# Seven products of quarter sums for 44 weight units of the two retention layers

## The chip, the cores and the metric

One core of one Trainium2 chip. The metric is the device time of one execution in microseconds; 1887.9 is the median of three runs of the kernel before (1887.67 to 1889.9).

## What is computed

512 tokens of width 1024 go through one block of differential attention, gated convolution and a feed-forward part, and then through two retention layers. Only the retention layers are touched:

```python
for layer in range(DEPTH_2):                                   # 2
    h = rms_norm(x, pre_norm[layer])
    proj = jnp.einsum("bsd,dp->bsp", h, w_in[layer])            # 1024 -> 8192
    c_b, c_c, c_x, c_z, r_q, r_k, r_v, r_z = jnp.split(proj, cuts, axis=-1)
    y_conv = c_b * causal_depthwise_conv(c_c * c_x, conv_w[layer])
    y_conv = y_conv * jax.nn.silu(c_z)
    q = apply_rotary(r_q...); k = apply_rotary(r_k...); v = r_v...
    ret = retention_chunkwise(q, k, v, log_gamma)
    ret = ret * lax.rsqrt(jnp.mean(ret * ret, axis=-1, keepdims=True) + NORM_EPS)
    y_ret = ret.reshape(b, s, D_RET) * jax.nn.silu(r_z)
    mix = jnp.concatenate([y_conv, y_ret], axis=-1)
    x = x + rms_norm(jnp.einsum("bse,ed->bsd", mix, w_out[layer]), post_norm[layer])
```

All of it is float32.

## The kernel before

Every large matrix product is done with split operands: a float32 value is written as a high part (a rounded copy, made by ScalarE) and a low part (the value less its high part, made by VectorE), and a product is the three matmuls high x high, high x low and low x high, with operands of 128 x 128 (held) and up to 128 x 512 (moving).

**Weights.** `plan` lists units of 1024 x 256 weights, each loaded by SyncE in one DMA of 1 MB into one of three buffers RAW. A unit is cut into slots (BY_COL: two halves of 128 columns; BY_K: two halves of 512 rows). `split_hi` (ScalarE) and `split_lo` (VectorE) make a slot's two parts in WHI and WLO, of which there are three places, taken in turn. A slot can be split once the slot that had its place before is `done`. `fill(upto)` splits as many slots as can be; `take` gives the next slot and fills two ahead. `load(u + 3)` follows the last split of unit u. Every queue is in order, and the order of the program is the order of each queue.

**A retention layer** is `layer(l)`, with four passes over p, each for two heads and 256 conv channels. A pass has three phases:
- q and k: `two_tiles` makes two tiles of 128 columns x 512 tokens each; ScalarE swaps halves into SW, VectorE does the rotation (two products and a sum per tile). In the first pass of the second layer `halves_qk` does this together with the end of the layer before.
- v and gate z (`fin`): 4 token tiles x 256 columns each, held operand the tokens, moving operand the weights; ScalarE writes VTK and SZ.
- The conv phase: kinds x, c, b, z, for each two tiles of 128 columns x 512 tokens, each tile read from PSUM by VectorE as soon as it is made. After each tile stands a piece of the attention (`pieces`: scores, states, mix_values, turn_back, in the second layer also turn_residual), and the elementwise work of the conv tile is emitted right behind it. Its result MXF is split at once into MXH and MXL; those of the attention are split in `turn_back`.

After the fourth pass the output projection multiplies MXH and MXL (`mix_out`, in the second layer `last_out`). `loose` is a list of small steps which are emitted at set points (`loose_run(n)`). PSUM has 8 banks, which turn over three roles.

The inner loop of a tile is in `products` (line 400), one matmul per instruction. A unit of two tiles is 2 x 8 x 3 = 48 matmuls of 512 moving columns; a unit of v or z is 96 of 256.

Of the kernel before, what the change touches and what calls it, by code (L numbers as in the profile page):

```python
# [52 lines left out]
def bass_diff_attention_block_then_retention_layers_kernel(  # L53
# [13 lines left out]
    KT = 8  # L67
# [13 lines left out]
    with ctx:  # L81
# [31 lines left out]

        con = [o_con]
# [75 lines left out]
        def mm(after, o, w, m, start, stop_, mark=False):  # L190
            return pe.put(after, lambda e: e.matmul(o, w, m, start=start, stop=stop_), mark)  # L191

# [100 lines left out]
        swaps, extra = [(1, 2)], {}  # L293
        for l in range(2):
            wl = w_in_2[l]
            for j in range(4):
                for g in (4, 5, 6, 7):
                    unit(cols(wl, 1024 * g + 256 * j), BY_K)
                for g in (2, 1, 0, 3):
                    unit(cols(wl, 1024 * g + 256 * j), BY_COL)  # L300
            if l == 0:
# [3 lines left out]


                n = sum(len(ss_) for _, ss_ in plan)
                extra[n - 1] = extra[n + 3] = 3
                swaps.append((n + 1, n + 2))
            else:  # L310
                for k in range(0, 16, 2):
                    unit(cols(w_out_2[l], 0, k, 2, 1024), [(0, 1, 0, 1024), (1, 2, 0, 1024)])

        raw_count = [Count(sem(f"raw{i}")) for i in range(3)]
        loaded, slots = [], []
# [5 lines left out]
        place = []  # L321
        for s in range(len(slots)):
            place.append(extra[s] if s in extra else (s - sum(e < s for e in extra)) % 3)
        before = [max((r for r in range(s) if place[r] == place[s]), default=None) for s in range(len(slots))]
        extra_free = []
        ready, gone = [], []

        def load(u, after):
            src = plan[u][0]
            n = src.shape[1] * src.shape[2]  # L330
            dst = RAW[u % 3][:, 0:n].rearrange("p (k c) -> p k c", k=src.shape[1])
            t = sp.dma(after, dst, src, raw_count[u % 3])
            loaded.append({k: t for k in range(src.shape[1])})

        def load_half(u, half):
# [4 lines left out]
            if half[0] == 0:  # L340
                loaded.append({})
            loaded[u][half[0]] = t

        halves = []

        def split_hi(s):
            u, (k0, k1, c0, c1), _ = slots[s]
            src = plan[u][0]
            n = (k1 - k0) * (c1 - c0)
            raw = RAW[u % 3][:, 0:src.shape[1] * src.shape[2]].rearrange("p (k c) -> p k c", k=src.shape[1])  # L350
            raw = raw[:, k0:k1, c0:c1]
            hi = WHI[place[s]][:, 0:n].rearrange("p (k c) -> p k c", k=k1 - k0)
# [4 lines left out]
            halves.append((hi, lo, raw, act([loaded[u][k0], used], hi, raw, ACT.Copy)))  # L357

        def split_lo(s):
            u, _, last = slots[s]  # L360
# [3 lines left out]
            if last and u + 3 < len(plan):  # L364
                load(u + 3, [t_lo])
# [14 lines left out]
        def fill(upto):  # L380
            while len(ready) < min(upto, len(slots)) and (before[len(ready)] is None or before[len(ready)] < len(gone)):
                split(len(ready))

        def fill_hi(upto):

            while len(halves) < min(upto, len(slots)) and (before[len(halves)] is None or before[len(halves)] < len(gone)):
                split_hi(len(halves))

        def done(token):
            gone.append(token)  # L390
# [84 lines left out]
        def whole():  # L475
# [953 lines left out]
            MXH = at("mxh", [128, 16, T2], R, o_c)  # L1429
            MXL = at("mxl", [128, 16, T2], R, o_c + 32768)  # L1430
# [56 lines left out]
            def layer(l):  # L1487
# [40 lines left out]
                def final_norm(f, a):  # L1528
                    t_pa[0] = t_x[f] = stt([a, t_x[f], t_w, xtok[f]], H[:, f, NM:T1], H[:, f, NM:T1], cv[:, f, WFIN:WFIN + 1], SUM4, ALU.mult, ALU.mult)
# [5 lines left out]
                mtok = [None] * 16  # L1535
                qk_used, vz_used, xa_used = {}, [], [dg_read, dg_read]
                sw_used = [extra_done, extra_done]

                for p in range(4):

                    b1, b2, b3 = roles
                    b4 = [6, 7]
# [496 lines left out]
```

How the kernel before makes its waits and increments, by code:

```python
    def play(self, eng):  # L41
        reached = {}
        for after, emit, sem, by in self.ops:
            for count, value in after:
                if reached.get(id(count), 0) < value:
                    eng.wait_ge(count.sem, value)
                    reached[id(count)] = value
            instruction = emit(eng)
            if by:
                instruction.then_inc(sem, by)
# [1933 lines left out]
        @block.sync  # L1984
        def _(eng):
            sp.play(eng)
            for count, value in finished:
                eng.wait_ge(count.sem, value)
```

## Time and profile before

| | us |
|---|---|
| runs, median of three | 1887.9 (1887.67 to 1889.9) |
| profiled execution, span | 1885.5 |
| one full pass of the first layer | 97.36 |
| its phases: q and k / v and z / conv | 22.36 / 22.74 / 52.26 |
| one full pass of the second layer | 98.23 |

The span is the time from the first to the last instruction of the profiled execution. The median of the runs is 2.4 us longer. A stage's TensorE time is read from the window table (busy time of each engine in a stretch); a matmul's pace is read from the starts of its neighbours in the list of instructions in order of time, since the matmuls overlap and their ends are modelled. The same holds for VectorE and ScalarE: a record runs on a little while the next one starts. Some matmul records may be missing.

### The profile page before, as it was taken

To read this page: it belongs to the slowest core of one execution; us is meant where nothing else is said; L and a number is where in the kernel's file an instruction comes from. 1 tells how busy PE (TensorE), PEld (TensorE's weight loads), DVE (VectorE), ACT (ScalarE), POOL (GpSimd) and SP (SyncE) were. 2 spreads that over 40 slices of the span, in tenths; PEclk is the share of its full clock that TensorE was granted. 3 is DMA by queue.
4 is the path that set the end of the run, shared out by engine and by line. 5 is a ranking of instruction groups with operands and counts; after the bars stand their busy time and mean duration, and the time that the engine had idled before them with its cause. 6 is when DMAs were issued, how large, how long until landed. Compare 5 with 4: busy or idle time off the path is not lost.

```text
span 1885.5 us, 28594 instructions
## 1 busy us (share of the span) xinstructions
PE 1867.1 (99%) x12262; PEld 1688.0 (90%) x12262; DVE 1130.1 (60%) x2035; ACT 737.5 (39%) x1379; POOL 1.2 (0%) x9
## 2 busy tenths in 40 slices
PE   8999999999999999999999999999999999999998
PEld 7999999877899988998898989898899898989887
DVE  5888897577657753666746363636266636454534
ACT  6222333677634432344433333333245333333322
POOL 0000000000000000000000000000000000000000
PEclk9999999999999999999999999999999999999999
DMA  5222222101222223223323233322333232223131
GB/s 185 94 90 90 71 94 87 64 24 46 68 73 92 95 89 107 90 78 94 107 83 102 78 90 90 89 90 80 100 90 90 73 96 78 90 71 108 68 123 45
DMA packets 151837, 163.64 MB, mean 87 GB/s; under 512 B 3495, under 2 KB 148192, under 8 KB 151711
## 3 DMA queue, kind: packets, MB, share of 16 engines
q1 hardware_dynamic: 151694, 161.82, 27.1%
q8 instruction: 96, 1.57, 0.3%
q14 instruction: 31, 0.25, 0.0%
q10 hardware_dynamic: 16, 0.00, 0.0%
HBM read 159.71 MB, written 2.10 MB: 86 GB/s over the span
## 4 chain that ended last, share of the span: by engine, by line
PE 98%; ACT 1%; DVE 1%; DMA 0%; issue 0%; SPq 0%; DVEq 0%
PE ps L191 95%; PE ps L196 2%; ACT nhi L199 0%; DMA xt<-in_x_dram 0%; ACT p L199 0%; DVE ast L973 0%; ACT L199 0%; DVE p L210 0%; DVE wlo L202 0%; ACT whi L199 0%; DVE m L202 0%; ACT ps L199 0%; DVE ga L210 0%; SPq L38 0%; ACT rbc L199 0%
## 5 line engine op out<-in xcount | busy, mean ns | idle before, releaser
L191 PE MATMUL ps<-nhi,whi 128*128 128x256 f32 (+3 forms) x2528 | 682.2, 319 | 3.6 <-DVE nlo L202 2.1
L191 PE MATMUL ps<-nhi,wlo 128*128 128x256 f32 (+3 forms) x2528 | 673.4, 316 | 0.0
L191 PE MATMUL ps<-nlo,whi 128*128 128x256 f32 (+2 forms) x2400 | 637.6, 318 | 0.0
L202 DVE TENSOR_TENSOR wlo<-raw,whi 128x1024 fp32r<-128x1024 f32 (+2 forms) x308 | 365.0, 1189 | 349.7 <-ACT whi L199 349.1
L191 PEld LDWEIGHTS ps<-nhi,whi 128*128 128x128 f32 x2528 | 426.2, 189 | 35.8 <-DVE nlo L202 2.3
L191 PEld LDWEIGHTS ps<-nhi,wlo 128*128 128x128 f32 x2528 | 425.5, 189 | 32.2
L191 PEld LDWEIGHTS ps<-nlo,whi 128*128 128x128 f32 x2400 | 400.8, 189 | 29.1
L199 ACT ACTIVATE whi<-raw 128x1024 fp32r<-128x1024 f32 (+2 forms) x308 | 314.6, 1026 | 261.4 <-PE ps L191 261.0
L210 DVE SCALAR_TENSOR_TENSOR c<-u,cv,c 128x514 f32<-128x514 f32 x240 | 163.2, 748 | 0.0
L191 PE MATMUL ps<-wlo,nhi 128*128 128x256 f32 x512 | 81.6, 281 | 0.0
L191 PE MATMUL ps<-whi,nhi 128*128 128x256 f32 x512 | 81.6, 281 | 0.0
L191 PE MATMUL ps<-whi,nlo 128*128 128x256 f32 x512 | 81.3, 281 | 0.0
L199 ACT ACTIVATE y<-zr,cf 128x512 f32<-128x512 f32 x44 | 35.8, 816 | 113.4 <-DVE zr L202 113.4
L191 PEld LDWEIGHTS ps<-whi,nhi 128*128 128x128 f32 x512 | 70.0, 189 | 0.6
L191 PEld LDWEIGHTS ps<-wlo,nhi 128*128 128x128 f32 x512 | 69.8, 189 | 0.0
L191 PEld LDWEIGHTS ps<-whi,nlo 128*128 128x128 f32 x512 | 69.6, 189 | 0.0
L191 PE MATMUL ps<-alo,whi 128*128 128x512 f32 x176 | 68.5, 389 | 0.0
L191 PE MATMUL ps<-ahi,whi 128*128 128x512 f32 x176 | 68.5, 389 | 0.0
L191 PE MATMUL ps<-ahi,wlo 128*128 128x512 f32 x176 | 68.5, 389 | 0.0
L210 DVE SCALAR_TENSOR_TENSOR y<-zr,cf,y 128x512 f32<-128x512 f32 x88 | 65.9, 748 | 1.8 <-ACT y L199 0.3
L207 DVE TENSOR_SCALAR nx<-ss 128x4 f32<-128x4 f32 (+2 forms) x26 | 4.3, 164 | 102.6 <-ACT ones_d L199 93.9
L199 ACT ACTIVATE ones_d<-ps,osc 128x128 f32<-128x128 f32 x64 | 23.5, 368 | 93.5 <-PE ps L191 91.9
(267 smaller groups left out, 2171.7 us busy)
## 6 DMA issues: line engine op xcount, KB each, us to landing
raw<-in_w_in_dram SPq DMA_DIRECT2D x90, 1024.0 KB, 5.5
raw<-in_w_up_dram SPq DMA_DIRECT2D x22, 1024.0 KB, 5.0
raw<-in_w_out_dram SPq DMA_DIRECT2D x20, 1024.0 KB, 5.1
raw<-in_w_down_dram SPq DMA_DIRECT2D x8, 768.0 KB, 4.9
raw<-in_w_down_dram SPq DMA_DIRECT2D x8, 640.0 KB, 4.6
raw<-in_w_conv_out_dram SPq DMA_DIRECT2D x4, 1024.0 KB, 5.2
xt<-in_x_dram SPq DMA_DIRECT2D x4, 512.0 KB, 5.5
raw<-in_w_in_dram SPq DMA_DIRECT2D x4, 512.0 KB, 8.2
```

Source lines behind the costliest of these rows:

```text
L191: return pe.put(after, lambda e: e.matmul(o, w, m, start=start, stop=stop_), mark)
L196: return pe.put(after, lambda e: e.transpose(o, i, idn), mark)
L199: return ac.put(after, lambda e: e.activation(o, i, func, **kw))
L202: return dv.put(after, lambda e: e.tensor_tensor(o, a, b, op))
L207: return dv.put(after, lambda e: e.tensor_scalar(o, a, s1, s2, op0, op1))
L210: return dv.put(after, lambda e: e.scalar_tensor_tensor(o, a, s, b, op0, op1))
```

## The change

In both layers the units of q and k (but for the first pass) and of x, c, b and z are multiplied as two-by-two blocks: the 1024 rows in two halves (four blocks of 128 each), the 256 columns in two halves, and the 512 tokens in two halves. Seven products of 512 rows x 128 columns with 256 tokens, of sums of weight quarters with sums of token quarters, and sums of their results give the four result quarters. 44 units are done so: 4 + 6 + 6 + 6 in each layer. The units of v and gate z, and q and k of each first pass, stay as they are.

- A unit of this kind has four slots: SEVEN. One (`0:8, 0:128`) is split as it is loaded. For the others `quarter_sums` first makes four sums on VectorE, three of them in place in RAW, one in S1T. One slot (place 4, WHI[4]) has half size. The places are written out by hand (`place`) in place of taken in turn.
- S1T, WHI[4] and WLO[4] lie in the third RAW buffer, so in the retention layers two RAW buffers are left, and a load follows the last split of the unit before it in its buffer.
- `token_sums` makes, once a layer, four combinations of the token quarters, TF, splits them into THI and TLO; `final_norm` waits for these as it overwrites H.
- `seven` emits the products over three banks: A takes four products and B one and C two, with accumulation carried on over what the bank already holds. Between products ScalarE copies the bank to SBUF (s1, u2, k5, u3, c21) and VectorE joins (c11, c22, c12). Two sets of three banks alternate; the attention has banks 6 and 7.
- Results of a unit now lie in SBUF, not in PSUM. The elementwise work of q, k and the conv kinds, also the rotation, is cut into steps in `loose`, and is emitted two steps at a time in `hook(m)` after each product; the attention's pieces stand at fixed hooks (`pieces`, key 7n + m).
- MXF shares its memory with the token sums, so mixed tiles stay float32 until the end of the last pass. `mix_split` makes their MXH and MXL: 8 tiles in z of the fourth pass, 8 at the start of the output projection.

The core of the diff:

```diff
+        SEVEN = [(0, KT, 0, 128, 0), (0, 4, 0, 128, 1), (0, 4, 0, 256, 2), (4, 8, 0, 256, 3)]
+        SEVEN_AT = [0, 4, 1, 2]
...
+        def quarter_sums(u):
...
+            w11, w21, w12, w22 = raw[:, 0:4, 0:128], raw[:, 0:4, 128:256], raw[:, 4:8, 0:128], raw[:, 4:8, 128:256]
+            t1 = tt([loaded[u][0], summed.get("split"), ready[-1][2]], S1T, w21, w22, ALU.add)
+            t3 = tt([t1], w21, w11, w21, ALU.add)
+            t2 = tt([t1, t3], w11, w11, S1T, ALU.add)
+            t4 = tt([t2], w12, w12, w11, ALU.add)
+            summed[u] = {1: t1, 2: [t2, t3], 3: t4}
...
+                    t = product(A, ah[:, 0:4, :], al[:, 0:4, :], ta, direct(0, TWO[0]), True, True, claim(banks[0]))
+                    s1 = act([t, after[0]], d11, A, ACT.Copy)
+                    hook(0)
+                    t = product(B, ah[:, 4:8, :], al[:, 4:8, :], ta, direct(1, TWO[0]), True, True, claim(banks[1]))
+                    done(t, s0)
+                    c11 = tt([t, s1], d11, B, d11, ALU.add)
+                    release(c11, banks[1])
+                    fill(s0 + 8)
+                    hook(1)
+                    t = t_used[0] = product(A, bh[:, :, left], bl[:, :, left], tb, summed_(0), False, True, s1)
+                    u2 = act([t], d12, A, ACT.Copy)
+                    hook(2)
+                    t = t_used[1] = product(C, ch, cl, tc, summed_(1), True, True, claim(banks[2]))
+                    done(t, s0 + 1)
+                    k5 = act([t, after[1]], d22, C, ACT.Copy)
+                    fill(s0 + 8)
+                    hook(3)
+                    t = t_used[2] = product(A, bh[:, :, right], bl[:, :, right], tb, summed_(2), False, True, u2)
+                    done(t, s0 + 2)
+                    u3 = act([t], d21, A, ACT.Copy)
+                    c22 = stt([k5, u3], d22, d22, -1.0, d21, ALU.mult, ALU.subtract)
+                    fill(s0 + 8)
+                    hook(4)
+                    t = product(C, dh[:, :, left], dl[:, :, left], td, direct(1, TWO[1]), False, True, k5)
+                    c12 = tt([t, u2], d12, C, d12, ALU.add)
+                    release(c12, banks[2])
+                    hook(5)
+                    t = t_used[3] = product(A, dh[:, :, right], dl[:, :, right], td, summed_(3), False, True, u3)
+                    done(t, s0 + 3)
+                    c21 = act([t, c22], d21, A, ACT.Copy, scale=-1.0)
+                    release(c21, banks[0])
+                    fill(s0 + 8)
+                    hook(6)
...
+                def mix_split(*ks):
+                    for k in ks:
+                        a = act([t_mx[k], t_used[k // 4]], MXH[:, k, :], MXF[:, k, :], ACT.Copy)
+                        mtok[k] = [a, tt([a], MXL[:, k, :], MXF[:, k, :], MXH[:, k, :].bitcast(F), ALU.subtract)]
...
+                    pieces = {1: lambda: scores(0), 4: lambda: states(0), 8: lambda: mix_values(0), 12: lambda: scores(1),
+                              15: lambda: states(1), 18: lambda: turn_back(0), 20: lambda: mix_values(1), 26: lambda: turn_back(1)}
...
+                        return [meet, tap0, lambda: tap(1), lambda: tap(2)]
...
+                        return [scale, gate, meet, last]
```

`product` does for k in 0 to 3 the three matmuls of 256 columns. `meet`, `tap(1)`, `tap(2)`, `scale`, `last` are VectorE, `tap0` and `gate` ScalarE.

## Rows read from the trace of the kernel before

**Rows 1.** The page: span, busy time and share, and the chain by engine.
```profile
span 1885.5 us, 28594 instructions
PE 1867.1 (99%) x12262; PEld 1688.0 (90%) x12262; DVE 1130.1 (60%) x2035; ACT 737.5 (39%) x1379; POOL 1.2 (0%) x9
...
PE 98%; ACT 1%; DVE 1%; DMA 0%; issue 0%; SPq 0%; DVEq 0%
```

**Rows 2.** Window table: a full pass, its phases; v/z of both layers' first pass.
```profile
core 0: us, PE busy (x) PEld busy (x) DVE busy (x) ACT busy (x) POOL busy (x), PEclk, DMA share, GB/s
937.51:962.04 24.53, 24.53 (x210) 24.52 (x208) 16.87 (x22) 9.91 (x19) 0.00 (x0) 1.00 0.35 106
...
1111.66:1134.02 22.36, 22.36 (x100) 18.11 (x98) 13.28 (x17) 9.10 (x13) 0.00 (x0) 1.00 0.39 113
1134.02:1156.76 22.74, 22.74 (x194) 22.74 (x192) 8.64 (x10) 8.33 (x17) 0.00 (x0) 1.00 0.31 95
1156.76:1209.02 52.26, 52.26 (x264) 43.74 (x263) 26.66 (x62) 16.94 (x37) 0.00 (x0) 1.00 0.24 73
...
1419.46:1443.09 23.63, 23.63 (x203) 23.63 (x202) 17.79 (x40) 11.80 (x22) 0.00 (x0) 1.00 0.28 84
...
1111.66:1209.02 97.36, 97.36 (x553) 84.59 (x552) 48.58 (x89) 34.38 (x65) 0.00 (x0) 1.00 0.29 87
```

**Rows 3.** TensorE in order of time: 256-column matmuls.
```profile
1134.02 0.63 PE L191 MATMUL ps<-whi,nhi 128*128 128x256 f32 x4
...
1145.38 0.64 PE L191 MATMUL ps<-whi,nhi 128*128 128x256 f32 x4
...
1372.03 0.28 PE L191 MATMUL ps<-mxh,wlo 128*128 128x256 f32 x1
...
1372.75 0.28 PE L191 MATMUL ps<-mxh,wlo 128*128 128x256 f32 x1
```

**Rows 4.** VectorE in order of time: starts of neighbouring operations.
```profile
1185.67 1.22 DVE L202 TENSOR_TENSOR wlo<-raw,whi 128x1024 fp32r<-128x1024 f32 x1
1186.81 0.69 DVE L202 TENSOR_TENSOR sd<-ps,far 128x512 f32<-128x512 f32 x1
1187.41 0.68 DVE L202 TENSOR_TENSOR pa<-ps,xa 128x512 f32<-128x512 f32 x1
...
1206.45 0.69 DVE L202 TENSOR_TENSOR xa<-xa,pa 128x512 f32<-128x512 f32 x1 [0.70 <-ACT pa L199]
1207.18 0.69 DVE L202 TENSOR_TENSOR mxf<-xa,rbc 128x512 f32<-128x512 f32 x1
...
1408.20 0.41 DVE L202 TENSOR_TENSOR h<-h,ox 128x256 f32<-128x256 f32 x1
1408.53 0.47 DVE L210 SCALAR_TENSOR_TENSOR nlo<-h,cv,nhi 128x256 fp32r<-128x256 f32 x1
```

**Rows 5.** TensorE and ScalarE in order of time: pick-up and four wide reads.
```profile
1176.86 0.47 PE L191 MATMUL ps<-nhi,whi 128*128 128x512 f32 x1
...
1156.61 1.57 ACT L199 ACTIVATE sz<-ps,ast 128x256 f32<-128x256 f32 x4 [4.28 <-PE ps L191]
...
1177.14 0.37 ACT L199 ACTIVATE ones_d<-ps,osc 128x128 f32<-128x128 f32 x1 [5.91 <-PE ps L191]
```

**Rows 6.** Who waited for whom, three full passes (1014 to 1306): total, times, longest.
```profile
DVE wlo L202 <- ACT whi L199: 53.1, 24, 6.2
DVE nx L207 <- ACT ones_d L199: 35.2, 6, 6.4
```

**Rows 7.** Weight loads of one pass: from issue to landing.
```profile
DMA to landing us min/median/max: 5.3/5.7/6.4
```

**Rows 8.** TensorE's clock: 264-column matmuls near the start; window table of the end.
```profile
13.32 0.42 PE L191 MATMUL ps<-nlo,whi 128*128 128x264 f32 x1
13.54 0.42 PE L191 MATMUL ps<-nhi,wlo 128*128 128x264 f32 x1
...
1870.00:1885.50 15.50, 9.17 (x41) 7.26 (x39) 10.93 (x29) 5.00 (x15) 0.00 (x0) 0.88 0.34 135
```

More of the change, by code:

```diff
@@ L191, in mm, with mm_on @@
             return pe.put(after, lambda e: e.matmul(o, w, m, start=start, stop=stop_), mark)
+        def mm_on(after, o, w, m, start, stop_, mark=False):
+            return pe.put(after, lambda e: e.matmul(o, w, m, start=start, stop=stop_, skip_group_check=True), mark)
         def tr(after, o, i, mark=False):
@@ L320, in bass_diff_attention_block_then_retention_layers_kernel @@
             slots[a], slots[b] = slots[b], slots[a]
-        place = []
-        for s in range(len(slots)):
-            place.append(extra[s] if s in extra else (s - sum(e < s for e in extra)) % 3)
+        assert len(place) == len(slots)
         before = [max((r for r in range(s) if place[r] == place[s]), default=None) for s in range(len(slots))]
+        pair_of = [b for b in ((first_layer + i) % 3 for i in range(3)) if b < 2]
+        rawbuf = [u % 3 if u < first_layer else pair_of[(u - first_layer) % 2] for u in range(len(plan))]
+        follows = [next((v for v in range(u + 1, len(plan)) if rawbuf[v] == rawbuf[u]), None) for u in range(len(plan))]
         extra_free = []
-        ready, gone = [], []
+        ready, gone = [], {}
         def load(u, after):
@@ L356, in split_hi @@
                 used = [gone[before[s]]]
-            halves.append((hi, lo, raw, act([loaded[u][k0], used], hi, raw, ACT.Copy)))
+            halves.append((hi, lo, raw, act([loaded[u][k0], used, summed[u][sums] if sums else None], hi, raw, ACT.Copy)))
         def split_lo(s):
-            u, _, last = slots[s]
+            u, box, last = slots[s]
             hi, lo, raw, t_hi = halves[s]
@@ L363, in split_lo @@
             ready.append((hi, lo, t_lo))
-            if last and u + 3 < len(plan):
-                load(u + 3, [t_lo])
+            if len(box) > 4 and box[4] == 1 or rawbuf[u] == 2:
+                summed["split"] = t_lo
+            if last and follows[u]:
+                load(follows[u], [t_lo])
         def split(s):
@@ L380, in fill, with done @@
         def fill(upto):
-            while len(ready) < min(upto, len(slots)) and (before[len(ready)] is None or before[len(ready)] < len(gone)):
+            while len(ready) < min(upto, len(slots)) and (before[len(ready)] is None or before[len(ready)] in gone):
                 split(len(ready))
         def fill_hi(upto):
-            while len(halves) < min(upto, len(slots)) and (before[len(halves)] is None or before[len(halves)] < len(gone)):
+            while len(halves) < min(upto, len(slots)) and (before[len(halves)] is None or before[len(halves)] in gone):
                 split_hi(len(halves))
-        def done(token):
-            gone.append(token)
+        def done(token, s=None):
+            gone[next(i for i in range(len(slots)) if i not in gone) if s is None else s] = token
         def products(slot, ks, xh, xl, xtok, dst, after, first, last, base=0):
@@ L1700, in layer @@
[L1700 to L1707 removed]
+                            loose_run(len(loose) if kind == "z" else 0)
@@ new lines, in layer, with hook @@
+                            dst, after = [PA[c][:, 2:TQ] for c in range(2)], [[t_pa[c], t_pad2, st["r2"], st["rb"]] for c in range(2)]
+                        def hook(m, n=n):
+                            if 7 * n + m in pieces:
+                                pieces[7 * n + m]()
+                            loose_run(2)
+                            if p == 3 and n == 3 and m >= 3:
+                                mix_split(*[None, None, None, (0, 1), (2, 3), (8, 9), (10, 11)][m])
+                        t = seven(dst, sets[n % 2], after, hook)
```

307 lines of the change are left out of this document (214 added, 93 removed).

## The prediction

> **What bounds the kernel now.** I read the page first. TensorE is busy 99% of the span, VectorE 60%, ScalarE 39% [rows 1], and the chain that ended last is TensorE for 98% of the span [rows 1]. So before the change nothing but the number and length of matmuls counts. Then the window table by stage. One of the later passes over p in a retention layer lasts 97.36 us; in it TensorE never stops and has its full clock (1.00 granted), VectorE works 48.58 us and ScalarE 34.38 us [rows 2]. The pass has three phases, which matter below because VectorE's work is uneven over them: q and k (22.36 us, VectorE 13.28), v and gate z (22.74, VectorE 8.64), and the four conv kinds with the attention pieces between them (52.26, VectorE 26.66) [rows 2]. The reader is to see that the conv phase leaves VectorE 25.6 us free and the v/z phase 14.1.
>
> **What the change takes from TensorE.** A unit is 256 output columns of q, k, x, c, b or z. Before, it is 2 tiles of 8 x 3 matmuls on 512 tokens. The q/k phase is 96 of them and little else in 22.36 us [rows 2], so 233 ns each and 11.2 us for a unit. After, it is 7 products of 4 x 3 matmuls on 256 tokens, 84 in all. 256-column matmuls are in the trace: from 1134.02 to 1145.38 96 of them stand, 118.3 ns each; three in a row into one bank (the new products put twelve) go by 120 ns (1372.03 to 1372.75, six of them) [rows 3]. At 119 ns a unit takes 10.0 us, so it saves 1.2 us, and 44 units (4 in the first pass and 6 in each of the three others, two layers) save 53 us; between 118.3 and 120 ns it is 50 to 55. If only TensorE counted, the median would go from 1887.9 to 1835. A half-width matmul costs almost exactly half, so the eighth of the work that seven products save is not eaten by TensorE itself.
>
> **What it gives to VectorE.** Prices are start-to-start where work is queued, since VectorE's records overlap: a split of 1024 elements whose successor is ready takes 1.14 us (1185.67 to 1186.81), an operation on 512 takes 0.60 (1186.81 to 1187.41); an operation that waits for the one before it takes 0.73 (1206.45 to 1207.18), 256 elements take 0.33 (1408.20 to 1408.53) [rows 4].
> - Splits of a unit: before 2 x 1.14 = 2.3. After 3 x 1.14 + 0.60 = 4.0 (four slots, one of half size).
> - Sums of weight quarters (quarter_sums): four of 512, each waiting for the last, 4 x 0.73 = 2.9.
> - Joining the products (c11, c22, c12): three of 256, 0.33 to 0.45 each, 1.1.
> That is 8.0 us in place of 2.3, plus 5.7 us a unit. The splits of the four mixed tiles (0.60 each) move out of each pass to the layer's end.
> The Trainium skill, "VectorE: DVE Perf Modes", section "The DRAIN you can't avoid", says that a semaphore between chained VectorE operations costs nothing extra. Rows 4 differ, 0.73 against 0.60; by the page the four sums would take 2.4 us instead of 2.9, and VectorE would get 3 us of each pass back.
>
> Set against TensorE's new time by phase: conv phase VectorE 26.66 + 4 x 5.7 = 49.5 us, TensorE 52.26 - 4 x 1.2 = 47.4. q and k: VectorE 13.28 + 2 x 5.7 - 1.8 (splits of mixed tiles gone) = 22.9, TensorE 20.0. v and z: VectorE about 10, TensorE 22.7. So a pass holds 80 us of VectorE in 90 of TensorE, but in the stretch from x to k it holds 72.4 against 67.4. The free time in v/z can't be used, as the weight slots and the operands for it don't exist yet. **This is the step that decides: the bound passes from TensorE to VectorE for three quarters of each pass.** If VectorE were never idle there, and 2 to 3 us of it were still unfinished when v begins, the stretch would take about 70 and the pass 92.5, 4.9 less than now.
>
> **Waits that are added.** Each later product takes the PSUM bank that ScalarE has just copied out (s1, u2, k5, u3). TensorE gives 1.4 us for each of these copies, the length of the product between. ScalarE picks up a TensorE result 0.28 us after the next matmul starts (1176.86 to 1177.14) and a 256-wide read takes 0.39 (four in 1.57) [rows 5], so there is 0.7 us to spare if ScalarE is free. But it works in order, and between the copies stand operations that wait for VectorE: the split of the summed slot (waits for t1), tap0 (waits for meet), gate (waits for scale), c21 (waits for c22). When VectorE runs late these hold u2, k5, u3 or the next s1, and TensorE waits for those. Also, each split on VectorE waits for ScalarE's half of it; now VectorE idles 53.1 us in three passes for that and 35.2 for the squares of mix_values, 24 and 6 times [rows 6]. A queue that is behind swallows most of it, not all. I followed the queues in order through the units. TensorE runs ahead of VectorE by at most about 1.5 us at t1 and 2 us at c22; VectorE still idles about 1.3 us where the A split stands behind tap0 or gate (in b and in q), 1.0 at each mix_values (four squares with their sums on ScalarE, then a chain of small steps on VectorE), and 1 to 2 at the start of x, where gate reads, two splits and s1 are queued together. Between nothing and 8 us a pass can be lost so; I take 4, near the hand sum, which gives 92.5 + 4 = 96.5, a gain of 1.0 of 97.36. Six passes: -6.
>
> **Once per layer.**
> - Token sums (token_sums): VectorE 8 x 0.40, two of 1024, four splits of 1024 or its like, 10.2 us. In the first layer they run from q on; VectorE has 16.87 of 24.53 us in v/z and earlier room [rows 2]: +1. In the second they can start only with v, where VectorE has 17.79 of 23.63 already [rows 2]; with 10.2 and the sums for x (3.4) it is 31.4. x needs the first of them: +8. If cover were perfect it would be 0, if x waited for all, 10.
> - First pass, conv phase: as above, about 0.
> - The last pass splits 8 mixed tiles inside z, 8 x 0.60 = 4.8 us on VectorE where it is the bound, and ScalarE as much: +4.5, twice.
> - z's epilogue is no longer ready when the output projection starts; its first part uses tiles split earlier and takes 5.5 us, so it mostly covers this: +1, twice.
> - Weight loads get two buffers in place of three. A load is issued with the last split of its buffer's old unit, about a unit and a half (15 us) ahead of its first split; one in this pass lands in 5.3 to 6.4 us [rows 7]: 0. If the lead were gone it would be 5 us a unit.
> - Extra ScalarE work, 3.4 us a unit, only counts through the waits above: ScalarE goes from 34 to about 55 of 90 us.
>
> Sum: -6 + 1 + 8 + 9 + 2 = +14 us. The profiled execution's span is 1885.5, 2.4 us below the median; both would rise alike. Predicted median 1887.9 + 14 = 1902.
>
> **Rivals.**
> - *VectorE's lateness is mostly absorbed* (faster). The pass reaches 92.5: -29 for six, -3 for each first pass' conv phase, and of the once-per-layer costs +5 is left: 1858. For it speaks that VectorE as a whole has room (80 in 90) and is idle today mainly for want of work; against it that the room lies in v/z.
> - *ScalarE's order stops both* (slower by more). One more us of waiting in each of five units per pass puts a pass at 101.5: +25, +6 for the first passes, +20 as above: 1939. It decides once VectorE is more than 2 us behind when t1 or c22 is due. For it: tap0, gate and swap stand in the very hooks ahead of the copies.
> - *TensorE's clock falls to its lower level, 1.2 GHz, because of the new stops.* Near the start TensorE did 264-column matmuls every 220 ns (13.32 to 13.54), double the later pace, and in the last 15.5 us, with TensorE busy 9.17, the granted clock is 0.88 [rows 8]. A unit in each pass at that pace costs 10 us: +80 on top, 1982. Against it: the stops I expect are 1 to 3 us among products. The Trainium skill, "TensorE: Matmul & The Clock Gate", section "A second HAM failure mode: psum-queue depth-cycling", tells of a kernel that lost its clock to short idles while it went round PSUM banks, which is the pattern here.
> - *The saving isn't there*: it needs a 256-column matmul at 134 ns or more; rows 3 exclude it nearly. 1955.
>
> **How the numbers follow.** Chances: forecast 0.45 (its own range 1882 to 1920), absorbed 0.29, ScalarE's order 0.20, clock 0.04, no saving 0.02. Of the forecast 0.06 lies below -0.2% and 0.09 within it. A measurement of this kernel tells about 0.2%, 3.8 us, from no change. Faster 0.29 + 0.06 = 0.35, same 0.10 with the edge of the first rival, slower 0.55. Range: 1848 (absorbed, with a further us saved per pass) to 1938.
>
> **What would show it.** In the profile after: 256-column matmuls within 118 to 121 ns of each other where they are not stopped; a unit with no stop at 10.0 us; VectorE busy above 75 us in a pass and above 90% from c to q; TensorE idle inside products 3, 5, 6, 7, released by ScalarE copies; passes of 95 to 98 us with v/z unchanged at 22.7; x of the second layer's first pass late by some 8 us; granted clock 1.00. I am wrong if passes take under 93 us (VectorE's lateness is absorbed) or over 100 (order), or if TensorE waits for weight loads.

## The result and the profile after

| | before | after |
|---|---|---|
| runs, median | 1888.9 (1887.67 to 1890.11, 4 runs) | 1956.97 (1954.74 to 1958.13, 4 runs) |
| ratio | | 1.036 [1.0346, 1.0376] |
| profiled execution, span | 1885.5 | 1954.2 |

Slower, as forecast, but by 68 us and not by 14 (69 by the spans): the time lies above the range (1848 to 1938).

The page of after, busy time and chain, against [rows 1]:

```profile
span 1954.2 us, 32772 instructions
PE 1861.4 (95%) x13846; PEld 1760.0 (90%) x13846; DVE 1385.4 (71%) x2461; ACT 903.4 (46%) x1731; POOL 1.2 (0%) x9
...
PE 77%; DVE 15%; ACT 5%; issue 2%; DMA 0%; DVEq 0%; SPq 0%; ACTq 0%
```

TensorE is busy for 6 us less (1867.1 before), in a span that is 69 us longer. So TensorE stands idle, and the chain now runs for a fifth over the two other engines. Where this happens is shown by the lengths of the stages, each from the start of its first matmul to that of the next stage (the profiled execution, us). A stage "x to k" is the conv phase of one pass with q and k of the next; v and z (22.76 in every full pass) are left out. In the first pass of layer 2 a stop at the start of x is counted with x.

| stage | before | after | order mended (e6_order) | the same, no sums (e7_ordns) | e11_first |
|---|---|---|---|---|---|
| up to the first retention layer | 913.48 | 923.65 | 913.89 | 913.42 | 913.86 |
| layer 1: its own q and k, v and z | 48.56 | 53.69 | 51.21 | 51.18 | 48.56 |
| first pass, x to k | 74.62 | 80.93 | 75.88 | 68.14 | 73.63 |
| second pass, x to k | 74.62 | 77.49 | 73.36 | 68.14 | 73.37 |
| third pass, x to k | 74.62 | 78.39 | 73.35 | 68.13 | 73.36 |
| fourth pass, conv | 52.26 | 51.75 | 50.24 | 48.10 | 50.24 |
| output projection, q and k of layer 2 | 113.08 | 125.32 | 113.00 | 112.92 | 113.04 |
| layer 2: v and z | 23.62 | 23.97 | 23.96 | 23.98 | 23.68 |
| first pass, x to k | 76.38 | 90.99 | 88.19 | 81.32 | 82.02 |
| second pass, x to k | 75.49 | 79.85 | 78.41 | 69.28 | 74.29 |
| third pass, x to k | 75.49 | 79.85 | 77.48 | 69.28 | 74.27 |
| fourth pass, conv | 53.15 | 58.24 | 51.52 | 49.26 | 51.55 |
| last output projection and end | 93.67 | 93.59 | 93.59 | 93.58 | 93.70 |

Window table of after (us; busy time of each engine with its instructions; granted clock): entry stop, v/z phase and x to k of the second pass of the first layer. The last two rows answer to the pass of [rows 2].

```profile
913.48:923.65 10.17, 2.71 (x13) 1.90 (x12) 6.53 (x12) 5.22 (x7) 0.00 (x0) 0.75 0.01 2
...
1058.27:1081.03 22.76, 22.76 (x195) 22.76 (x194) 11.88 (x15) 9.67 (x19) 0.00 (x0) 1.00 0.30 93
1081.03:1158.52 77.49, 71.22 (x577) 69.61 (x575) 66.41 (x123) 42.72 (x86) 0.00 (x0) 0.98 0.26 82
```

A pass is 100.25 us (97.36 before). VectorE works 66.4 of the 77.5 us from x to k, less than I had priced (72.4), and still TensorE stops for over 6. Who stops it, in that pass (total, times, longest):

```profile
PE ps L199 <- ACT mxf L207: 2.3, 1, 2.3
PE ps L199 <- ACT qr L207: 2.3, 1, 2.3
PE ps L199 <- ACT pa L207: 1.4, 1, 1.4
PE ps L199 <- DVE rcol L214: 0.2, 1, 0.2
```

Before, TensorE waited for nothing in such a pass. Now there are three long stops, and ScalarE ends each. The longest is inside unit b. TensorE, then ScalarE, then VectorE in order of time (start, length, engine, operation, in brackets the idle time before it and who ended it):

```profile
1114.44 0.60 PE L204 MATMUL ps<-ident,sz 128*128 128x128 f32 x4
1117.32 0.39 PE L199 MATMUL ps<-nhi,whi 128*128 128x256 f32 x1 [2.29 <-ACT mxf L207]
```

```profile
1116.28 0.72 ACT L207 ACTIVATE xa<-pa,cv 128x512 f32<-128x512 f32 x1 [3.43 <-DVE pa L210]
1116.91 0.36 ACT L207 ACTIVATE mxf<-ps 128x256 f32<-128x256 f32 x1
```

```profile
1113.59 0.61 DVE L210 TENSOR_TENSOR state<-ps,state 128x128 f32<-128x128 f32 x2
1114.11 1.53 DVE L218 SCALAR_TENSOR_TENSOR xa<-pa,cv,xa 128x512 f32<-128x512 f32 x2
1115.56 0.68 DVE L210 TENSOR_TENSOR pa<-pa,xa 128x512 f32<-128x512 f32 x1
1116.16 0.68 DVE L210 TENSOR_TENSOR s1t<-raw 128x512 f32<-128x512 f32 x1
```

The reader is to follow it backwards. TensorE needs the bank that `mxf<-ps` (k5) copies out. That copy takes 0.36 us, and its operand was made before the last product that TensorE did. But in ScalarE's queue it stands behind `tap0` of the second conv tile, which waits 3.43 us for `meet` of that tile; and `meet` (1115.56) stands on VectorE behind both taps of the first tile (1114.11). The steps of a tile are emitted one after the other (meet, tap0, tap, tap), so ScalarE's step of the second tile comes due only after VectorE has done four. VectorE is late here: in the 15.4 us up to the stop's end it is busy 13.8, ScalarE 7.1. The order passes VectorE's lateness on to the copy, and so to TensorE.

```profile
1101.90:1117.32 15.42, 13.01 (x105) 12.12 (x103) 13.77 (x25) 7.10 (x14) 0.00 (x0) 1.00 0.22 69
```

The same stop stands in q, where `gate` takes the place of `tap0`, and right behind it the clock (TensorE, first layer; the granted clock is in the windows below):

```profile
1043.84 0.36 PE L199 MATMUL ps<-nhi,whi 128*128 128x256 f32 x1 [2.25 <-ACT qr L207]
...
1044.99 0.42 PE L199 MATMUL ps<-nhi,whi 128*128 128x256 f32 x1
1045.20 0.42 PE L199 MATMUL ps<-nlo,whi 128*128 128x256 f32 x1
```

```profile
1043.84:1044.99 1.15, 1.15 (x10) 1.15 (x11) 1.08 (x3) 0.79 (x3) 0.00 (x0) 0.98 0.00 0
1044.99:1048.30 3.31, 3.31 (x18) 3.31 (x17) 3.27 (x6) 0.92 (x1) 0.00 (x0) 0.50 0.00 0
1048.30:1058.27 9.97, 9.97 (x85) 9.97 (x85) 8.31 (x13) 6.46 (x11) 0.00 (x0) 1.00 0.35 108
```

TensorE stood for 2.5 us, went on at 0.12 us a matmul, and 1.15 us later the granted clock is 0.50, the lower level (1.2 GHz of 2.4): a matmul every 0.21 us, 16 of them from 1044.99 to 1048.39 where 1.9 us would do (a window's count takes in those that reach over its ends). Then it is back. Such a stretch costs 1.5 us. Not every stop has one: behind the stop at 1117.32 the clock stays. After has 17 stretches at the lower level, 75.4 us together; before has one, at its end. Summed over the matmuls that start in them, each less its pace at full clock, they cost about 26 us (an estimate: steps that hold a stop are left out).

The entry stop, 7.46 us, is of another kind:

```profile
923.65 0.79 PE L195 MATMUL ps<-nhi,whi 128*128 128x512 f32 x1 [7.46 <-DVE wlo L210]
```

### The profile page after: what moved, and what is told of

Same layout as the page of the kernel before. It is cut to its first block, busy times and chain, and to the rows that moved or that the text cites. A ratio compares the mean times of both kernels' runs of the same rounds, so it can differ in the third digit from the quotient of the medians.

```text
span 1954.2 us, 32772 instructions
## 1 busy us (share of the span) xinstructions
PE 1861.4 (95%) x13846; PEld 1760.0 (90%) x13846; DVE 1385.4 (71%) x2461; ACT 903.4 (46%) x1731; POOL 1.2 (0%) x9
## 4 chain that ended last, share of the span: by engine, by line
PE 77%; DVE 15%; ACT 5%; issue 2%; DMA 0%; DVEq 0%; SPq 0%; ACTq 0%
PE ps L195 63%; PE ps L199 12%; DVE wlo L210 4%; PE ps L204 2%; ACT ones_d L207 2%; ACT whi L207 1%; DVE raw L210 1%; DVE pa L210 1%; DVE xa L218 1%; DVE sz L218 1%; DVE xa L210 1%; DVE na L210 1%; DVE na L218 1%; DVE rcol L218 1%; DVE s1t L210 1%
## 5 line engine op out<-in xcount | busy, mean ns | idle before, releaser
L210 DVE TENSOR_TENSOR wlo<-raw,whi 128x1024 fp32r<-128x1024 f32 (+1 forms) x352 | 417.1, 1192 | 335.8 <-ACT whi L207 334.8
L207 ACT ACTIVATE whi<-raw 128x1024 fp32r<-128x1024 f32 (+1 forms) x352 | 359.7, 1032 | 227.8 <-PE ps L195 205.4
L195 PE MATMUL ps<-nhi,whi 128*128 128x256 f32 (+3 forms) x1824 | 401.0, 288 | 11.1 <-DVE wlo L210 7.7
L195 PE MATMUL ps<-nhi,wlo 128*128 128x256 f32 (+3 forms) x1824 | 397.4, 286 | 0.0
L195 PE MATMUL ps<-nlo,whi 128*128 128x256 f32 (+3 forms) x1696 | 360.1, 286 | 0.0
L199 PE MATMUL ps<-thi,whi 128*128 128x256 f32 x704 | 209.4, 298 | 9.4 <-DVE wlo L210 4.4
L199 PE MATMUL ps<-tlo,whi 128*128 128x256 f32 x704 | 203.6, 289 | 0.0
L199 PE MATMUL ps<-thi,wlo 128*128 128x256 f32 x704 | 203.5, 289 | 0.0
L199 PE MATMUL ps<-nhi,whi 128*128 128x256 f32 x528 | 154.7, 293 | 30.9 <-ACT mxf L207 18.3
L199 PE MATMUL ps<-nhi,wlo 128*128 128x256 f32 x528 | 151.7, 287 | 0.0
```

The source lines that it names most:

```text
L207: return ac.put(after, lambda e: e.activation(o, i, func, **kw))
L210: return dv.put(after, lambda e: e.tensor_tensor(o, a, b, op))
```

## The experiments

All ratios are to the kernel before on the same chip. The edits of one experiment apply to the kernel after unless another is named.

**Where the stops come from: three repairs, one at a time.** The last slot of the feed-forward part and the first of the retention layers now share weight place 0, so the first cannot be split before the second is done. e1_entry renames the three places from the retention layers on; the two RAW buffers stay.

```diff
+        place = [p if s < 2 * first_layer or p > 2 else (p + 1) % 3 for s, p in enumerate(place)]
```

> The changed kernel, with the three weight places renamed in a ring (0 to 1, 1 to 2, 2 to 0) from the first slot of the retention layers on; nothing else. In the changed kernel the last slot of the feed-forward part and the first slot of the retention layers both have place 0, so the first can't be split before the last matmul that uses it, and TensorE stands 7.85 us at the entry, then runs 10.2 us at the lower clock. Theory 'place': the stop goes, and with it the lower clock there: 8 to 11 us less than the changed kernel's 1957. Rival 'two RAW buffers' (the load comes late): the stop stays, 0.

Measured: 1940.86, ratio 1.0275 [1.026, 1.029], 16 us below after, more than the 8 to 11 expected. Of the 16.5 us between the two profiled executions 10.1 are the stop and the lower clock behind it, 2.6 a fall of the clock near 375 that only after's has (more on it below), and the rest lies in later stages where the clock fell in other places. TensorE goes over into the layer without a stop:

```profile
913.27 0.39 PE L195 MATMUL ps<-ahi,wlo 128*128 128x512 f32 x1
913.49 0.39 PE L195 MATMUL ps<-nhi,whi 128*128 128x512 f32 x1
```

So the stop came from the name of a place. The loads, with two buffers, are not its cause. The stretch of 10.2 us at the lower clock that began in this stop, and slowed q and k by 2.5 us, is gone with it.

e2_inter emits the steps of the two tiles of c, and of z, in turn, so that both VectorE steps (meet, or scale) lie ahead of both ScalarE steps (tap0, or gate):

```diff
-                                loose.extend(c_out(c, t[c], fs[c]))
+                                if c:
+                                    s0_, s1_ = [c_out(i, t[i], fs[i]) for i in range(2)]
+                                    loose.extend([s0_[0], s1_[0], s0_[1], s1_[1], s0_[2], s0_[3], s1_[2], s1_[3]])
```

> The changed kernel with the steps of the two conv tiles interleaved: meet, meet, tap0, tap0, then the other taps; scale, scale, gate, gate, then the rest. Same work, but ScalarE's tap0 and gate are queued one hook after the VectorE step that they wait for. Theory 'ScalarE's order': the two or three stops of 2.5 us per pass (k5 behind tap0 in b, the copies behind gate in q) and the lower clock after them go: 3 to 5 us for each of seven passes, 20 to 35 in all. Theory 'VectorE is the bound': the same work takes the same time, the stops only move: under 8 us.

Measured: 1925.39, ratio 1.0194 [1.0177, 1.0211], 32 us below after, with the same work on every engine. Second pass, TensorE's waits from x to k, and the window:

```profile
PE ps L199 <- ACT pa L207: 1.4, 1, 1.4
PE ps L199 <- DVE rcol L214: 1.2, 1, 1.2
...
PE ps L199 <- ACT mxf L207: 0.2, 1, 0.2
```

```profile
1075.85:1149.21 73.36, 69.70 (x577) 68.25 (x575) 66.00 (x123) 42.70 (x86) 0.00 (x0) 1.00 0.28 87
```

The wait for `mxf` falls from 2.3 to 0.2, the stretch from 77.49 to 73.36, and the clock stays at 1.00.

e5_out is about the start of the first output projection. There TensorE stopped twice (4.79 and 3.49 us from start to start). ScalarE, in order of time:

```profile
1337.25 1.28 ACT L207 ACT_TABLE_LOAD   x1
...
1340.52 1.28 ACT L207 ACT_TABLE_LOAD   x1
1341.81 0.63 ACT L207 ACTIVATE pa<-pa 128x512 f32<-128x512 f32 x1
...
1345.07 1.99 ACT L207 ACTIVATE whi<-raw 128x1024 fp32r<-128x1024 f32 x2
1346.96 2.17 ACT L207 ACTIVATE mxh<-mxf 128x512 fp32r<-128x512 f32 x4
```

A square root, put there to have its table ready, now stands ahead of the last gates of z, so the table is changed twice, and the splits of the mixed tiles follow just as TensorE wants them. The edit moves the square root behind the gates, and each of the two groups of four splits two weight slots ahead.

```diff
-                t_e = act([vset([], nst[:, 0:1], 1.0)], nst[:, 1:2], nst[:, 0:1], ACT.Sqrt)
...
+                        mix_split(*range(4, 8))
+                        t_e = act([vset([], nst[:, 0:1], 1.0)], nst[:, 1:2], nst[:, 0:1], ACT.Sqrt)
...
-                            if n in (1, 3):
-                                mix_split(*range(4 * n, 4 * n + 4))
+                            if i == 1:
+                                mix_split(*range(12, 16))
```

> The changed kernel with the start of the first layer's output projection put in another order: the Sqrt that warms ScalarE's table after the last gates and not before them, and the last 8 mixed tiles split one slot earlier. Same work. In the changed kernel this stage is 12.2 us longer than before the change, with stops of 4.4 and 3.1 us that end with mxl, and 10.2 us at the lower clock. Theory 'order of these queues': both stops and the clock's fall go, 8 to 12 us. Rival 'the work of splitting all 16 tiles at once is too much for VectorE and ScalarE': under 4 us.

Measured: 1939.17, ratio 1.0272 [1.0258, 1.0286], 18 us below after; the stage goes from 125.32 to 114.45. The profiled execution took 1945.13, 6 us more than the three others; it lies 11 us below after's, nearly all of it in this stage. Where the others gain 6 more is not shown (their mean clock is 0.987, its own 0.982).

**All order together.** e6_order has these three and two more for the second layer: `stats_out(7)`, whose matmuls stood ahead of x and waited 4.1 us for ScalarE's copies of v, moves into the first unit, and the two `turn_residual` stand one product earlier and one later. e10_nob has them at products 22 and 27.

```diff
-                        pieces[22] = lambda: turn_residual(p, 0, r1, t_t)
-                        pieces[24] = lambda: turn_residual(p, 1, r1, t_t)
+                        pieces[21] = lambda: turn_residual(p, 0, r1, t_t)
+                        pieces[25] = lambda: turn_residual(p, 1, r1, t_t)
```

> All changes of order together, no work removed: weight places renamed at the entry, conv tiles' steps interleaved, output projection's start, and in the second layer the norm's broadcast after x's first product and the residual's turns at other hooks. Theory 'order was the loss': the parts add, 10 + 27 + 10 + about 15 in the second layer, so 1957 - 62 = 1890 to 1900, the kernel before within 0.7%; the passes stay at 96, set by VectorE. Rival 'order gives all of it': the stretch x to k falls to 68 and the time to 1850.

> The same changes of order with all 44 units as seven products, so that only the mixing is left between the two. In the order kernel before, each pass of the second layer has a stop of 3.5 us at turn_back of the second head, behind the residual's turn; it should go: 1904 - 3 x 3 = 1893 to 1898. If the stop has another cause, it stays at 1904.

Measured: e6_order 1904.42, ratio 1.0077 [1.0064, 1.009]; e10_nob 1895.71, ratio 1.0036 [1.0024, 1.0049]. Some 61 of the 68 us are gone with not one operation fewer. In the second layer the place of the residual's turn is worth 4.1 us in the second pass (78.41 against 74.30): with 21 and 25 its transposes wait 3.2 us at one point for a copy in ScalarE's queue, with 22 and 27 TensorE's longest wait in that stretch is 0.8.

**What the quarter sums cost.** e3_nosum leaves them out of the kernel after, e7_ordns out of e6_order:

```diff
-            t1 = tt([loaded[u][0], summed.get("split"), ready[-1][2]], S1T, w21, w22, ALU.add)
-            t3 = tt([t1], w21, w11, w21, ALU.add)
-            t2 = tt([t1, t3], w11, w11, S1T, ALU.add)
-            t4 = tt([t2], w12, w12, w11, ALU.add)
+            summed[u] = {1: None, 2: None, 3: None}
```

> The changed kernel without the four sums of weight quarters of each unit; the slots are split from the quarters as loaded (this leaves out part of the computation). It takes 2.9 us of 8.0 off VectorE's work for a unit and leaves ScalarE's order as it is. Theory 'VectorE is the bound': the stretch from x to k falls from 77.5 us to near TensorE's 67.4, 8 to 10 us a pass, 65 to 85 in all, so to 1870 to 1890. Theory 'ScalarE's order': tap0 and gate still stand before the copies and wait for VectorE steps; stops get shorter but stay, 20 to 40 in all.

> The kernel with all changes of order, and without the sums of weight quarters (this leaves out part of the computation). Theory 'with the order mended VectorE is the bound': now the 2.9 us a unit show in full, 4 to 6 us a pass, 30 to 45 us less than the same kernel with the sums, so about 1850. Rival 'sums are hidden': within 8 us of the kernel with them.

Measured: e3_nosum 1926.24, ratio 1.0199 [1.0184, 1.0214], 31 us below after. e7_ordns 1856.15, ratio 0.9825 [0.981, 0.984], 48 us below e6_order. So the sums cost more where the order is good; where it is bad, half of what they take is hidden under stops that come anyway. Windows of the second pass, x to k, in e6_order and in e7_ordns:

```profile
1063.73:1137.09 73.36, 69.72 (x576) 68.26 (x575) 65.98 (x123) 42.76 (x86) 0.00 (x0) 1.00 0.29 87
```

```profile
1055.50:1123.63 68.13, 68.09 (x576) 67.89 (x575) 53.35 (x103) 42.98 (x86) 0.00 (x0) 1.00 0.30 94
```

In e7_ordns TensorE waits for nothing, and 68.13 is what its own work takes. In e6_order the same work takes 5.2 us more, and the waits of VectorE's operations in that window are all told these:

```profile
DVE wlo L210 <- ACT whi L207: 5.7, 2, 4.8
DVE nx L215 <- ACT ones_d L207: 1.7, 2, 1.1
DVE qr L210 <- ACT sw L207: 0.4, 1, 0.4
```

VectorE is idle for 7.4 of the 73.36 us, and the one long wait (4.8) ends at 1066.12, so 2.4 of them are its end. From there on VectorE is idle for 5.0 of 71.0 us, and never for long. So with order mended the sums on VectorE are what holds TensorE up. Leaving them out takes away two things, though, VectorE's work and ScalarE's wait for it (the split of a sum), and this pair of runs can't tell them apart.

**GpSimd instead.** e4_pool makes the four sums on GpSimd, which is idle.

> The changed kernel with the four sums of a unit made by GpSimd, which is idle otherwise, in place of VectorE. Same arithmetic. If GpSimd takes under about 2 us for each of the four additions (8 of the 10 us of a unit) it is hidden, and the time is that of the kernel without the sums, 1870 to 1900; if its operations are slower or hold up VectorE's, GpSimd becomes the bound: at 3 us each 12 us a unit, and the time rises to 2000 or more.

Measured: 2052.19, ratio 1.085 [1.0818, 1.0882], 95 us above after. GpSimd takes 1.34 to 1.54 us for an addition of 512 (VectorE 0.69), so the four take 5.4 to 7.2 from first to last, and the stretch from x to k grows to 89.8 us. And VectorE is slowed beside it. A group of VectorE from x to k of the second pass, in after and then in e4_pool (busy, mean ns of one | idle before):

```profile
L210 DVE TENSOR_TENSOR mxf<-xa,rbc 128x512 f32<-128x512 f32 x2 | 1.4, 691 | 0.1
```

```profile
L210 DVE TENSOR_TENSOR mxf<-xa,rbc 128x512 f32<-128x512 f32 x2 | 2.3, 1165 | 0.1
```

The 1165 is the mean of two different operations. In order of time, GpSimd and VectorE in e4_pool:

```profile
1132.20 1.29 POOL L372 TENSOR_TENSOR s1t<-raw 128x512 f32<-128x512 f32 x1 [14.03 <-DVE wlo L210]
...
1165.17 1.56 POOL L372 TENSOR_TENSOR s1t<-raw 128x512 f32<-128x512 f32 x1 [6.27 <-DVE wlo L210]
```

```profile
1131.95 0.61 DVE L210 TENSOR_TENSOR state<-ps,state 128x128 f32<-128x128 f32 x2
1132.47 1.57 DVE L218 SCALAR_TENSOR_TENSOR xa<-pa,cv,xa 128x512 f32<-128x512 f32 x1
...
1164.92 0.69 DVE L210 TENSOR_TENSOR xa<-xa,pa 128x512 f32<-128x512 f32 x1
1165.64 1.64 DVE L210 TENSOR_TENSOR mxf<-xa,rbc 128x512 f32<-128x512 f32 x1
...
1172.62 0.69 DVE L210 TENSOR_TENSOR mxf<-xa,rbc 128x512 f32<-128x512 f32 x1
```

An operation with two operands in SBUF that starts while an addition runs on GpSimd takes longer, `mxf<-xa,rbc` by about 1 us: 1.64 us in all 6 such cases of this trace, 0.69 in the 10 others. Where one operand is in PSUM (`state<-ps,state`), the 8 that start beside an addition take 0.29 us, as elsewhere. The Trainium skill, "GPSIMD Engine Reference", section "1. Specifications", says that GpSimd shares its SBUF interfaces with VectorE and that they contend where a VectorE instruction has two SBUF inputs; this trace agrees, with 1.64 against 0.69 us. Part of the 95 us is the clock: its stretches at the lower level last 199.9 us together (75.4 in after) and cost, counted as above, some 65 us against 26.

**The clock by itself.** e8_warm leaves the order as it is and lets TensorE do idle matmuls, which add to a part of a bank that is overwritten, at the long stops in b, in q and at the residual.

```diff
+                    for _ in range(warm):
+                        mm_on(claim(banks[1]), P[:, 512 * banks[1] + 256:512 * banks[1] + 512], THI[1][:, 0, 0:128], THI[1][:, 1, :], False, True)
```

> The changed kernel with idle matmuls put where TensorE stands in each pass: 8 of 256 columns ahead of the sixth product in b and in q, 12 ahead of the second turn of the residual; their results go to a part of PSUM that nobody reads. They take 1.0 and 1.4 us inside stops of 2.5 and 3.8. Theory 'the lower clock comes from these stops and costs 1.1 to 2 us each time': some 8 of the 15 falls go, and 8 to 14 us with them. Rival 'the clock costs nothing that the stops did not': 0, or up to 10 us more where the matmuls don't fit into the stops.

Measured: 1946.24, ratio 1.0301 [1.0287, 1.0315], 10.7 us below after; the mean clock of its profiled execution is 0.989 (0.981), and the cost of the lower level, counted as above, falls from 26 to 13 us. So the clock is a loss of its own, but one that follows from the stops: in e10_nob, which has no idle matmuls, it is 0.994.

**Fewer units with seven products.** If VectorE is the bound, a unit that is multiplied whole should pay for its 1.2 us of TensorE. e9_mixed does so (on e6_order, with the residual as in e10_nob) for b in all passes, and for x and c too in the first pass of layer 2. e11_first does so for all conv kinds and z of each first pass, so that the token sums are due only a pass later, and spreads their steps over that pass (36 units stay). e12_firstb adds b in all passes to that, with `mix_values(1)` three products earlier and `turn_back(0)` two later. Each has its kinds in one line:

```diff
+        def whole_kinds(l, p):
+            return 'xcbz' if p == 0 else ''
```

> All changes of order (the residual's second turn now after the last product of z), and the unit of b in every pass, and x, c and b in the second layer's first pass, multiplied whole again, with 48 matmuls of 512 columns and one ScalarE copy per tile. That gives back 1.2 us of TensorE's saving for each of 10 units (44 become 34) and takes 5.7 us of VectorE's work off each. Theory 'VectorE is the bound from x to k': the stretch falls from 73.4 to 69 or 70 us although TensorE has more to do, and the time to 1860 to 1872, below the kernel before. Rival 'seven products always pay': with fewer of them the time rises by 12 us to 1915.

> Order mended as in e10_nob, and in the first pass of each retention layer the conv kinds and z are multiplied whole, as in the kernel before; all other units (36) have seven products. The token sums are then due only with the second pass and are spread over the first. Theory (the first passes lose because token sums, square sums and quarter sums meet in them on VectorE): the conv phase of the first pass goes from 77.4 to about 75 us in the first layer and from 87.0 to 76 to 79 in the second, the other passes stay at 73.4 and 74.3 from x to k; time 1878 to 1887, so 0 to 10 us under the kernel before. Rival (VectorE is behind everywhere, and a first pass that is done earlier only meets the same work later): the second passes lengthen by what the first ones gain, time 1892 to 1897.

> As e11_first, and b is multiplied whole in every pass too (30 units with seven products), with mix_values(1) in the last third of b and turn_back(0) after it. It saves VectorE 5.7 us a pass and costs TensorE 1.2. Theory (VectorE is the bound from x to k with some 73.4 us, TensorE alone would need about 68): the stretch falls to 70 to 72, the time to 1865 to 1877. Rival (as in e9_mixed, the freed time of VectorE can't be used, since b's weight halves come late and the chain of mix_values(1) moves work into z): the stretch stays at 73 to 76, and the time is that of e11_first or up to 8 us more.

Measured: e9_mixed 1904.27, ratio 1.008 [1.0066, 1.0094]. e11_first 1884.73, ratio 0.9984 [0.9975, 0.9993]. e12_firstb 1894.49, ratio 1.0031 [1.002, 1.0042]. e11_first went as its theory had it, but for the second layer's first pass, 82.0 instead of 76 to 79: two stops of 2 us stay there, at the transposes of k and of the residual, and which of VectorE's work they go back to was not isolated. The others did not: e9_mixed is 8.6 us above e10_nob, which has all 44 units, and e12_firstb 9.8 above e11_first. Second pass of e12_firstb, the window, and who waited on VectorE and on TensorE:

```profile
1058.88:1133.96 75.08, 71.78 (x540) 68.66 (x539) 61.04 (x114) 40.89 (x81) 0.00 (x0) 0.98 0.28 85
```

```profile
DVE wlo L210 <- ACT whi L207: 12.4, 5, 4.8
...
PE ps L199 <- ACT pa L207: 2.3, 1, 2.3
PE ps L199 <- ACT kr L207: 0.6, 1, 0.6
```

VectorE has 5.0 us less to do than in e11_first (66.00), but it now waits 12.4 us for ScalarE's halves, where it waited 5.7, and the stretch is 1.7 us longer. The time is set free in b, where the next weight slots can't be split yet, and is missing in z, where the stop for `pa` grows from 1.4 to 2.3 us and the clock falls once. A count of busy time over the pass doesn't show that. So VectorE's amount of work alone does not set the pass, even with order mended; the handing over between it and ScalarE does in part. e9_mixed, with `mix_values(1)` three products later, has the same 75.08 us in its second pass; no further order of b was tried.

## Why the prediction was wrong, step by step

**TensorE's saving: right, a little too large.** In after, undisturbed 256-column matmuls of the new products follow one another by 119 ns:

```profile
1125.28 0.28 PE L199 MATMUL ps<-tlo,whi 128*128 128x256 f32 x1
...
1127.67 0.28 PE L199 MATMUL ps<-thi,whi 128*128 128x256 f32 x1
```

(20 steps in 2.39 us). From x to k I had 67.4 us for TensorE and e7_ordns shows 68.13, against 74.62: 1.1 us a unit, not 1.2. The rival that the saving isn't there is excluded.

**VectorE's price: slightly too high.** The four sums do follow by 0.72 us as priced: 1116.16, 1116.88, 1117.61, 1118.33. (The rule of the Trainium skill, "VectorE: DVE Perf Modes", section "The DRAIN you can't avoid", that a semaphore in a chain costs nothing, which I had set against rows 4, is not borne out: the split behind them, which does not wait for the last sum, comes after 0.61.) A pass holds 66.4 + 11.9 = 78.3 us of VectorE. I had written 80, but my own terms, 72.4 and about 10, add up to 82.

**The decisive step, that the bound passes to VectorE: half right.** For the mended kernel it holds as far as it was tested: its pass takes 73.36 + 22.76 = 96.1 us, where I forecast 96.5, and leaving out the sums brings TensorE's own 68.13; but e9_mixed and e12_firstb, which take 5 us off VectorE, gain nothing, so the bound is not VectorE's work alone, and the near hit on 96.5 is in part luck. For the kernel as given, whose pass takes 100.25, it misses what comes on top: its longest stops are made by the order in which ScalarE's copies stand behind steps that wait for VectorE, and e2_inter takes 4.1 us of them from the pass (77.49 to 73.36) with the same work. "ScalarE's order stops both" was a rival with a chance of 0.20 and a price of 1939. Its mechanism, its place (tap0 and gate ahead of the copies) and its engine were right, and as it had it, passes went over 100. It should have been the forecast. What I did wrong is the hand sum. I followed the queues, found VectorE waiting for ScalarE, and took 4 us for a pass. The case in which TensorE waits for a copy queued behind a ScalarE step that waits for VectorE I named, but gave no price of its own in that sum. One check would have done: of each step that stands ahead of a copy, what has VectorE to do before it? For `tap0` of the second tile this is `meet`, `tap`, `tap`, `meet`, and it comes due in the product in which k5 is wanted.

**Terms, against what the stages show** (14 forecast, 68.7 measured by the spans; the lower clock is in each):

| term | forecast | measured |
|---|---|---|
| later passes, with the last pass' splits (-6 + 9) | +3 | +19.9 |
| first passes: token sums and conv phases | +9 | +23.9 |
| starts of the output projections | +2 | +12.2 |
| entry to the first retention layer | 0 | +12.7 |

The entry I had covered under "weight loads with two buffers: 0". The loads were indeed not the cause (they land in 5.3 us, as in [rows 7]). I had looked at the buffers and not at the places, which the change writes out by hand; e1_entry shows that cost. Of the 12.7, 7.6 are the stop, 2.5 the clock in q and k, and the rest is a fall of the clock near 375, in a part that the change leaves alone. It is in some profiles (e2_inter, e9_mixed) and not in others (e1_entry, e6_order), so this part is not put down to the change. At the output projection I had taken "mostly covered" without looking at what ScalarE has in its queue there. The first pass of layer 2 came late, as forecast (+8), but by 14.6. The splits of mixed tiles in the last pass (+4.5 twice) hardly cost anything: the fourth conv phase is 51.75 in the first layer (52.26 before), and 48.10 in e7_ordns, which has them too, where TensorE's saving alone would give 47.4; in the second layer it is 58.24, but 51.52 with order mended.

**The clock.** I gave 0.04 to it and 1982 to its case, by whole units at the lower level, and argued that stops of 1 to 3 us among products would leave it alone. They did not: of the 24 stops of 2.2 us and more in the retention layers, 15 have a fall of the clock in them or right behind them, most of some 3.4 us. What the Trainium skill, "TensorE: Matmul & The Clock Gate", section "A second HAM failure mode: psum-queue depth-cycling", tells of a clock lost to short idles between banks is borne out in kind. The price is some 26 us and not my 80, as each fall is short. It adds to any other case and is no case of its own: without it the time would be near 1931, inside the range (so it would without the 25 us of the entry and the output projection). The order rival's 1939 with 26 us for the clock gives 1965, and the median is 1957, but that is near in the sum only: the 25 us of the entry and the output projection were in neither.

**The steps that failed, in short.** The waits that are added, 4 us a pass, left out TensorE's wait for copies behind tap0 and gate (4.1 us of the second pass, by e2_inter); entry and output projection were put at 0 and +2 without looking at the weight places and at ScalarE's queue (12.7 and 12.2); and the clock's falls behind stops were put at nothing (some 26 us, spread over all of these).

## What to carry to other kernels

When an elementwise chain alternates between two engines and one of them also has to free banks for TensorE, price each copy by everything that stands ahead of it in its queue and by what those wait for, on the other engine's queue too. Emit the chains of two tiles in turn. And where a change stops TensorE again and again, add a price for the clock (here 15 of 24 stops of 2.2 us and more had a fall, of some 1.5 us each); sum up what the mended version would bring before judging the idea (here 61 of 68 us were order, and what is left of the idea is a tie, 0.9984 at best).

## What was not expected of the hardware

- A single stop of TensorE of 2.5 us can be followed by some 3.4 us at the lower level (0.50 granted; 213 against 119 ns for a 256-column matmul, so about 1.5 us lost), which begins about 1 us after it goes on. In after such a fall stood in or behind 15 of 24 stops of 2.2 us and more. Stops of the same length differ: of the two of 2.56 us in unit b, at 1016.17 and at 1117.32, the first has one and the second none. Behind the stops of 1.4 and 1.6 us of the first layer in e2_inter there was none.
- GpSimd additions of 128 x 512 float32 take 1.34 to 1.54 us. A VectorE operation with two SBUF operands that starts while one runs takes longer (`mxf<-xa,rbc` 1.64 against 0.69 us); `state<-ps,state`, with one operand in PSUM, is not slowed (0.29 us).
